# A two-layer mLSTM/retention block: modulation sums dealt out over the steps of a head, gate rows moved behind the first loads

## The reference, cut to what matters

```
ada = silu(c) @ w_ada[l] + b_ada[l]              # 1024 -> 3072: shift, scale, gate
h = rmsnorm(x) * (1 + scale) + shift
p = h @ w_in[l]                                  # mq mk mv mo mz | i f | rq rk rv rz
li, lf = i, log_sigmoid(f);  b = cumsum(lf) in chunks, m = running max
mlstm: 4 heads of 256, chunkwise, with the rows b, m, li - b as weights
retention: 4 heads of 256, chunkwise, with fixed decays and rotary q, k
x = x + gate * (concat(y_m, y_r) @ w_out[l])
```

## Time and profile before

| | |
|---|---|
| time, median of 3 | 3663.46 us (3662.02 to 3663.48) |
| the profiled execution | 3658.34 us, span 3656.4 us |
| mean granted TensorE clock | 0.939 |
| TensorE (PE) busy | 3319.2 us, 91% |
| weight loads (PEld) | 2229.8 us, 61% |
| VectorE (DVE) | 1461.8 us, 40% |
| GpSimd (POOL) | 1443.9 us, 39% |
| ScalarE (ACT) | 833.6 us, 23% |
| chain of waits | PE 80%, DVE 11%, ACT 3%, POOL 3% |

### The profile page before, as it was taken

The page is one execution under the profiler, slowest core; times in us unless marked ns, Lnnn a source line. Parts: engine busy times, 40 slices in busy tenths (PEclk is TensorE's granted clock), DMA queues, the critical chain, the costliest instruction groups (busy, mean ns, idle before and its releaser), DMA issues.

```text
span 3656.4 us, 37413 instructions
## 1 busy us (share of the span) xinstructions
PE 3319.2 (91%) x13893; PEld 2229.8 (61%) x13893; DVE 1461.8 (40%) x2466; ACT 833.6 (23%) x1477; POOL 1443.9 (39%) x1372
## 2 busy tenths in 40 slices
PE   5999887899999989996799997989999989999998
PEld 4665553556666555453444445877897468889953
DVE  6121428744334321235742324454553233344332
ACT  2211313631111031212531102323111023321110
POOL 0008989920000000999100004776553047776600
PEclk6999897899999999988899998999999999999998
DMA  5111010003333111201013321222232222122211
GB/s 189 46 35 35 18 35 23 1 24 98 93 92 97 38 46 46 52 24 35 1 58 124 124 91 58 81 93 93 81 105 69 71 70 65 62 70 79 72 40 53
DMA packets 259174, 236.40 MB, mean 65 GB/s; under 512 B 20870, under 2 KB 257202, under 8 KB 258996
## 3 DMA queue, kind: packets, MB, share of 16 engines
q1 hardware_dynamic: 258996, 234.02, 20.9%
HBM read 231.90 MB, written 2.10 MB: 64 GB/s over the span
## 4 chain that ended last, share of the span: by engine, by line
PE 80%; DVE 11%; ACT 3%; POOL 3%; issue 2%; DMA 0%; DVEq 0%; ACTq 0%; SPq 0%; POOLq 0%
PE ps L406 34%; PE ps L894 20%; PE ps L436 11%; DVE arena L1425 3%; ACT arena L1036 2%; DVE arena L1429 2%; PE ps L944 2%; DVE arena L1431 2%; PE ps L584 2%; PE ps L643 1%; PE ps L422 1%; PE ps L677 1%; PE ps L656 1%; PE ps L988 1%; DVE arena L1427 1%
## 5 line engine op out<-in xcount | busy, mean ns | idle before, releaser
L406 PE MATMUL ps<-hT,wring 128*128 128x512 f32 (+1 forms) x1568 | 573.7, 525 | 2.5 <-ACT arena L1036 2.5
L406 PE MATMUL ps<-arena,wring 128*128 128x512 f32 (+1 forms) x1280 | 491.9, 545 | 10.6 <-DVE arena L1425 10.6
L406 PEld LDWEIGHTS ps<-hT,wring 128*128 128x128 f32 x1568 | 299.5, 192 | 264.0 <-issue 245.6
L1943 POOL TENSOR_TENSOR arena<-wring 128x512 f32<-128x512 f32 x72 | 93.7, 1302 | 916.1 <-DMA wring<-in_w_in 608.3
L1907 POOL TENSOR_TENSOR arena<-arena,posi 128x512 f32<-128x512 f32 (+1 forms) x360 | 412.9, 1147 | 30.0
L436 PE MATMUL ps<-hT,wring 128*128 128x512 f32 (+1 forms) x1088 | 422.2, 542 | 0.0
L406 PEld LDWEIGHTS ps<-arena,wring 128*128 128x128 f32 x1280 | 243.4, 192 | 247.8 <-issue 228.4
L1036 ACT ACTIVATE arena<-ps 128x256 f32<-128x256 f32 (+4 forms) x435 | 187.4, 431 | 735.2 <-PE ps L406 306.7
L1425 DVE TENSOR_TENSOR arena<-arena 128x768 f32<-128x768 f32 (+7 forms) x141 | 183.1, 1298 | 384.4 <-ACT arena L1036 380.9
L436 PEld LDWEIGHTS ps<-hT,wring 128*128 128x128 f32 x1088 | 207.7, 196 | 185.8 <-issue 176.6
L1036 ACT ACT_TABLE_LOAD x148 | 189.9, 1283 | 491.4 <-PE ps L514 97.7
(11 more groups left out here) (177 smaller groups left out, 4450.2 us busy)
## 6 DMA issues: line engine op xcount, KB each, us to landing
wring<-in_w_in SPq DMA_DIRECT2D x128, 1024.0 KB, 5.3
wring<-in_w_mod SPq DMA_DIRECT2D x24, 1024.0 KB, 7.8
wring<-in_w_out SPq DMA_DIRECT2D x24, 1024.0 KB, 5.6
wring<-in_w_ada SPq DMA_DIRECT2D x24, 1024.0 KB, 5.2
wring<-in_w_conv_out SPq DMA_DIRECT2D x8, 512.0 KB, 3.5
wring<-in_w_gla_out SPq DMA_DIRECT2D x8, 512.0 KB, 4.0
wring<-in_w_attn_out SPq DMA_DIRECT2D x8, 512.0 KB, 4.0
arena<-in_x SPq DMA_DIRECT2D x1, 2048.0 KB, 9.7
```

The lines of the kernel that those rows point to most:

```text
L406: last = eng.matmul(o_(out), a, b_, start=(i == 0), stop=(i == len(parts) - 1))
L1943: pool.link(eng.tensor_tensor(t1, w[:, 0:4, P:2 * P], w[:, 0:4, 0:P], ALU.subtract))
```

## The change

`steps2` puts both of a head's modulation places elsewhere: group 2n - 3 is finished and group 2n - 2 is loaded after corners 1, group 2n - 2 is finished and 2n - 1 loaded after corners 3. On VectorE the eight sums become a generator: `mod load` only sets it up, each later `products` step takes two instructions of it, each `scores`, `values` and `turn` step one, after its own work, and `mod` takes what is left. In both layers of the block ScalarE makes its three functions of the f gate after the first `u1` of the layer; VectorE runs the scans after its part of corners 0 of head 0, and the other five row operations after that of corners 1.

```
--- before.py
+++ after.py
@@ steps2, proj(n) @@
             yield [("load", n, i), ("products", n, i)]
             mods = []
-            if i == 0 and 2 <= n < 8:
-                mods = [("mod", n, 2 * n - 3)]
-            elif i == 2 and 1 <= n < 7:
-                mods = [("mod load", n, 2 * n - 2)]
+            if i == 1:
+                mods = ([("mod", n, 2 * n - 3)] if 2 <= n < 8 else []) + ([("mod load", n, 2 * n - 2)] if 1 <= n < 7 else [])
             elif i == 3 and 1 <= n < 7:
                 mods = [("mod", n, 2 * n - 2), ("mod load", n, 2 * n - 1)]
             yield [("corners", n, i)] + mods
@@ scalar @@
-                fn(rM[0:4, :], rF[0:4, :], ACT.Abs)
-                fn(rM[0:4, :], rM[0:4, :], ACT.Exp, scale=-1.0)
-                fn(rM[0:4, :], rM[0:4, :], ACT.Ln, ("f ln", l), bias=1.0)
...
                         fn(U1, bank_of["left", k][:, 0:HALF], ACT.Copy, ("u1", k))
+                        if (n, x[0]) == (0, 0):
...
+                            fn(rM[0:4, :], rF[0:4, :], ACT.Abs)
+                            fn(rM[0:4, :], rM[0:4, :], ACT.Exp, scale=-1.0)
+                            fn(rM[0:4, :], rM[0:4, :], ACT.Ln, ("f ln", l), bias=1.0)
@@ vector @@
             def modulate(L, g):
+                for _ in mod_by_product(L, g):
+                    pass
+
+            def mod_by_product(L, g):
...
                     ts(sums, w[:, 0, :], cT[:, col0 + 8 * c:col0 + 8 * c + 1], None, M_, None)
+                    yield
                     for k in range(1, KD):
+                        dve.stage("modulation")
                         stt(sums, w[:, k, :], cT[:, col0 + 8 * c + k:col0 + 8 * c + k + 1], sums, M_, A_,
                             ("mod summed", L, g) if (c, k) == (ncol - 1, KD - 1) else None)
+                        yield
                 mods_done.append((L, g))
...
+                summing = iter(())
                 for kind, n, *x in steps2():
                     if kind == "mod load":
                         if l < DEPTH - 1:
-                            dve.stage("modulation")
-                            modulate(L + 1, x[0])
-                            dve.stage("cell")
+                            summing = mod_by_product(L + 1, x[0])
+                    elif kind == "mod":
+                        for _ in summing:
+                            pass
+                        dve.stage("cell")
...
+                    if kind in ("products", "scores", "turn", "values"):
+                        for _ in range(2 if kind == "products" else 1):
+                            next(summing, None)
+                        dve.stage("cell")
+                    if (kind, n) == ("corners", 0):
+                        if x[0] == 0:
+                            gate_scans()
+                        elif x[0] == 1:
+                            gate_rows()
```

More of the change, by code:

```diff
@@ L1362, in _ @@
                         fn(U1, bank_of["left", k][:, 0:HALF], ACT.Copy, ("u1", k))
+                        if (n, x[0]) == (0, 0):
+                            act.stage("cell_gates")
+                            fn(rM[0:4, :], rF[0:4, :], ACT.Abs)
+                            fn(rM[0:4, :], rM[0:4, :], ACT.Exp, scale=-1.0)
+                            fn(rM[0:4, :], rM[0:4, :], ACT.Ln, ("f ln", l), bias=1.0)
+                            act.stage("cell")
                     elif kind == "corners":
@@ L1745, in _, with gate_scans, gate_rows @@
                 tt(hsum[3], quarter[0][1], hsum[1], S_, ("h sums", l))
-                dve.stage("cell_gates")
                 R = slice(0, 4)
                 v3 = lambda x_: x_[R, :].rearrange("p (a b) -> p a b", b=CH)
[L1749 to L1758, removed]
+                def gate_scans():
+                    dve.stage("cell_gates")
+                    eng.wait_ge(*at(("f ln", l)))
+                    eng.wait_ge(*at(("free", ("if", l))))
+                    stt(rF[R, :], rF[R, :], 0.0, rM[R, :], ALU.min, S_)
+                    dve.link(eng.tensor_tensor_scan(rM[R, :], rF[R, :], rI[R, :], 0.0, A_, ALU.max))
+                    dve.link(eng.tensor_tensor_scan(rB[R, :], gscan[R, 0:TX], rF[R, :], 0.0, M_, A_))
+                    dve.stage("cell")
+                def gate_rows():
+                    dve.stage("cell_gates")
+                    tt(rU[R, :], rB[R, :], rM[R, :], S_)
+                    tt(rW[R, :], rI[R, :], rB[R, :], S_)
+                    cp(small[R, 33:36], rM[R, CH - 1:TX - 1:CH])
+                    tt(v3(rI), v3(rU), small[R, 32:36].unsqueeze(2).broadcast_to([4, NCH, CH]), A_)
+                    tt(v3(rF), v3(rW), rU[R, CH - 1:TX:CH].unsqueeze(2).broadcast_to([4, NCH, CH]), A_, ("gate rows", l))
+                    dve.stage("cell")
                 dve.stage("cell")
```

## The result

The changed kernel takes 3707.7 us (median of 4 runs, 3705.72 to 3714.52) beside 3662.7 us of the kernel before on the same chip (3661.4 to 3663.48): a ratio of 1.013, 95% interval 1.0118 to 1.0143, so it is slower: by 45 us by the medians, by 48 by the ratio. 3709 was forecast. The profiled execution's span grew by 47.5 us, from 3656.4 to 3703.9, at the same mean clock (0.939 and 0.938).

A forecast was written before the change was run, and what follows sets the result against it. TensorE, busy 91% of the span and 80% of the chain, was taken as the bound. Heads +7, +40, +4 and +11 made +62, gates -16: +46 on the median's 3663.5 gives 3709 us, range 3695 to 3722.

The forecast's parts named there:

- head 1: Third layer: the last projection load waits for the first modulation load's eighth sum; next scores 0 7 us later.
- heads 2, 3: Third layer: the third and last projection loads come late and TensorE waits 10.6 us for `modT`; +20 us each.
- heads 4 to 7 (turn, W0, W2): Third layer: turn delayed 2 us, next heads' first and third projection loads held by modulation sums; +4 and +11 us.
- gates, both layers: Head 0 of both layers: gaps before the first corners and their slow restarts go; -16 us, between -10 and -17.
- The sums as owners of a slot: Third layer's four-slot load ring: unfinished modulation sums keep slots, so later projection loads wait; +62 us over the heads.
- both holds: Heads 2 and 3: first modulation load holds the last projection load; the second holds the next head's third; +20 us each.
- (a): Rival: only the last projection load is late, so heads 2 and 3 lose 7 us each; 3683 us, chance 0.18.
- (b): Rival: ring slots come free before GpSimd wants them, so the kernel is faster; -36 us, 3628 us, chance 0.10.
- (c): Rival: a wash, heads 1 to 3 lose 5.5 us each, without the retention heads' and turn's waits; 3663, chance 0.04.
- (d): Rival: the sums block GpSimd too, 5 us in each late run of three heads; +15 on top, 3724, chance 0.07.

The follow-up runs named there:

- the second load at once: The changed kernel with the second modulation load of each head summed at once and only the first dealt out: 3680.1 us, ratio 1.0065 to the kernel before.
- the bias ahead of the silu: The changed kernel with ScalarE adding the odd groups' bias in corners 1 before the silu of tile 0: 3694.2 us, ratio 1.0098 to the kernel before.
- the gates alone: The changed kernel with modulation steps in their old places, all eight sums at once, gates' work still moved: 3648.4 us, ratio 0.9967 to the kernel before.

## Why the prediction was right, and where it was off

By heads, from scores 0 to scores 0 (us); head 0, where the gates are, from its first product. All are differences of the two profiled executions:

| term | forecast | measured |
|---|---|---|
| head 1 | +7 | +6.0 (84.2 to 90.2) |
| heads 2, 3 | +20, +20 | +16.4, +19.2 |
| heads 4 to 7 (turn, W0, W2) | +15 | +14.9 |
| gates, both layers | -16 | -9.8 (75.0 and 76.4 to 70.8) |
| everything else | 0 | +0.7 |
| sum | +46 | +47.5 |

**What held.** The sums as owners of a slot: W4 of head 1 reached GpSimd at T + 62.2 (forecast 63.8). In head 2 A was issued at T + 17.0 (18.8), W2 reached GpSimd at T + 25.4 (28), TensorE waited 10.78 us for `modT` (10.6), A was done at T + 68.0 (70), and the next scores 0 came at T + 101.2 (104.2). That the wait for `modT` came out so close is two misses that cancel: the taps were done 2.6 us earlier than forecast, but silu and bias took 2.7 us behind them and not 1.1, since a table load of 1.28 us stands in front (2427.59), and TensorE reached its wait 1.4 us earlier. That both holds cost what they were said to is shown by the second load at once, which ends one of them alone, and by the bias ahead of the silu, which ends the ScalarE link. In the retention heads the waits for W0 and W2 were 1.59 and 1.92 us (2.3 and 3.1); heads 5 and 6 still grew by 4.0 and 5.9 us where 5.4 each were forecast, and heads 4 and 7 by 3.0 and 2.0 where it was 4 and nothing. So the good sum of this row is in part luck. How the growth splits between turns and restarts is not shown.

**What was mis-sized.** Heads 2 and 3 were put 4.4 us too high together in the sum: B's eighth sum came 1.8 us earlier than I had it, and W4 reached GpSimd 5.3 us after A, not 6.1. (For those 6.1 the forecast names, which has 6.3.)

**What was wrong.** The step "The scans and row operations are covered by VectorE's idle time between corners 0 and the next u2, and between corners 1 and the one after. If they don't fit beside GpSimd's work, a microsecond or two comes back each time." The gaps gave what was forecast: from the first product to GpSimd's first pair sum it is 12.5 us in both layers, for 20.1 and 21.5 before, so -7.6 and -9.0, -16.6 together. But GpSimd's chain, which sets the end of head 0, grew by 3.4 us in each layer under VectorE's operations of 4 partitions (56.5 to 59.9), 6.8 of the 16.6, and the gates' term came out just outside its range of -10 to -17. I had asked whether VectorE had room and not what its operations do to GpSimd. The only row at hand on that, of the modulation sums, had 0.06 us per operation; beside a scan it is 0.8. The two misses, -5 in the heads and +6 in the gates, nearly cancel: that the total is better than its terms is luck.

The Trainium skill, "SBUF — State Buffer", section "SBUF: two separate sides", has the shared port pair as an exclusive lock under which the loser is fully blocked. By that rule GpSimd's operation beside a scan would be late by what is left of the scan. When the operations at 2243.30 and 2245.44 began, 1.0 us of a scan was left each time, and the 0.8 us added to 1.27 is near that; the 0.06 beside the modulation sums is not, and here too the measurement decides.

**The rivals.** (a) would have been 3683: heads 2 and 3 show W2 late as well. It is near what the second load at once makes of the kernel (3680). (b) fell with A's eighth sum at T + 68. One thing it was given for it was misread: in the earlier trace rows VectorE is busy 43.7 of 84 us, 52%, and so not idle for more than half of the head. With all sums at once both slots come free in time, but then VectorE's gap is there too: that is the gates alone, -12 and not -36. (c) fell with heads 2 and 3 and with the 14.9 us of the retention heads. (d) looked for the lengthening in the wrong place: GpSimd's late run of head 2, from 2462.14 to the end of its last tap, took 27.0 us with three sums beside it, for 27.3 before with eight. It was the gates' operations that lengthened GpSimd's.

## What to carry to other kernels

A reader of a ring slot is an owner of it: before its work is spread over idle time, write down when its last instruction now ends and which load is behind that slot in the queue's order, and what that load's reader then holds up. Spreading sums of 0.5 us to close a gap of 4.8 us held W4 and W2 back by 9 to 20 us in the first two mLSTM heads. Idle time of one engine is only free if its instructions don't lengthen those of an engine on the path. The version that beats both kernels is the gates alone, 12 us below the kernel before in each of two comparisons (7 to 18 and 7 to 16).

## What the runs showed of the hardware

VectorE operations of only 4 partitions lengthen GpSimd's nearly as much as they are lengthened: a scan of 4x512 from 1.21 to 2.20 us and GpSimd's 128x512 sum from 1.27 to 2.06. All of a layer's gate operations together lengthened a run of GpSimd without a gap from 56.5 to 59.9 us. VectorE's modulation sums of 128x256 are lengthened (0.52 to 1.25) but hardly lengthen GpSimd's (1.30 to 1.36). Why the two kinds differ is open.
